# Hybrid decoder trunk on eight cores: convolution matrices cast in DRAM, the finished tile stored and reloaded in pairs of blocks, four transposes moved by one score

## The chip, the cores and the metric

The kernel runs on all 8 cores of one Trainium2 chip. Each core computes one of the 8 sequences of the batch and exchanges nothing with the others. The metric is the device time of the slowest core in microseconds (us), from its first to its last instruction with what lies around it. On each core TensorE (PE in the profile) multiplies matrices, VectorE (DVE), ScalarE (ACT) and GpSimd (POOL) work elementwise, and SyncE (SP) only issues DMAs. POOL issues DMAs too. Transfers issued by SP go through one hardware queue (q1), those issued by POOL through one software queue (q0); only the latter can change the type on the way, as from float32 to bfloat16.

## The reference

```python
def mixer_block(u, w_in, conv_a_w, conv_b_w, conv_b_bias, ln_b_g, ln_b_b, w_out):
    z = jnp.einsum("bsd,de->bse", u, w_in)
    b_a, c_a, h_a, v_b, g_b = jnp.split(z, [D_A, 2 * D_A, 3 * D_A, 3 * D_A + D_B], axis=-1)
    y_a = b_a * causal_dwconv(c_a * h_a, conv_a_w)               # 3 taps
    glu = v_b * jax.nn.sigmoid(g_b)
    cb = causal_dwconv(glu, conv_b_w) + conv_b_bias              # 31 taps
    y_b = jax.nn.silu(layer_norm(cb, ln_b_g, ln_b_b))
    return jnp.einsum("bse,ed->bsd", jnp.concatenate([y_a, y_b], -1), w_out)

h = x                                                            # (8, 4096, 1024) float32
for l in range(2):
    h = h + mixer_block(rms_norm(h, norm_mix_g[l]), ...)
    h = h + memory_cross_attention(rms_norm(h, norm_x_g[l]), rms_norm(mem, norm_mem_g[l]), ...)
    h = h + sqrelu_mlp(rms_norm(h, norm_ffn_g[l]), w_up[l], w_down[l])
return rms_norm(h, final_g)
```

The attention has 4 heads over 256 memory tokens; the MLP is 4096 wide.

## The kernel before

**Tiling.** A core's 4096 positions are cut into four tiles of 1024, each of two halves `s` of 512 positions. The outer loop runs over tiles ("passes" 0 to 3), the inner one over the two layers. The residual stream of the tile lies in `h[0]` and `h[1]`, 8 blocks of 128 channels by 512 positions in float32, 2 MB each. For one tile and one layer the stages are `mixer`, `attend`, `ffn_up` and `ffn_down`.

**Mixer.** It multiplies for the gates and values (`gv_part`), for c and h (`ch_part`), in the order gv 0, ch 0, gv 1, ch 1, each 8 groups of 8 matmuls of 512 columns. After gv 1 the gated values `glu` are laid out anew by 16 small SBUF to SBUF DMAs (line 814, 8 on SP and 8 on POOL) into `glc`, in which four phases of the positions lie on the partitions; ch 1 runs beside that. Then comes the 31-tap convolution: 8 matrices of 128x2304 (the conv matrices), 144 matmuls of 256 columns, all of which read `glc`. The layer norm and SiLU follow on DVE and ACT, and their output goes back to channel order in another 16 small DMAs per half (line 865) into `ycat`; meanwhile PE does the 8 groups of b, and then the first half of the output projection (`out_half`), whose second half needs `ycat`.

**Weights.** All weights pass through a ring of 10 slots in SBUF (`ring_pump`), in the fixed order `seq`. A slot is reloaded when the PE work on it is done. The large weights are read as float32 and cast on the way by POOL's DMAs (line 442). Some matrices are prepared once, in pass 0, kept in the DRAM tensor `wbf` in bfloat16, and read from there by SP (line 448): the folded attention matrices that `setup(l)` computes, and the conv matrices. A `wbf` matrix is loaded only once its store has been issued. In pass 0 the conv matrices of layer 0 are built in SBUF by DVE out of the taps, and those of layer 1 are cast from `bands` by POOL; in both layers each matrix is then stored to `wbf` by SP (`wb_store`, line 469), right after the layout DMAs of line 814 in SP's order. These stores use two semaphores in turn, and a store waits until the one before it on its semaphore has landed.

**Order of the work.** Each engine's instructions stand in the order in which the Python code emits them, and each waits only for what it needs. `tick()` is called once per group of 8 matmuls; each tick runs one entry of the background list `bg` and one step of each unfinished `spawn`ed task. At the end of a tile `fin(s)` computes the scale `RC[s]` of the final norm and appends 8 entries to `bg`, one for each block's multiply on DVE (line 1076), and a ninth, `final_store`: it stores the 2 MB of `h[s]` in one DMA, and issues one 2 MB DMA that reloads `h[s]` with x of the next tile, which waits for the store. `fin(0)` comes at the last tick of the tile and `fin(1)` four ticks later, so these entries run in the mixer of the next tile. The first norm of the next tile does not need `h`: it reads x through two staging buffers earlier on.

**Attention.** The scores `Sc(s, i)` (8 per half, 8 matmuls of 512 columns each) go through a softmax on DVE, ACT and POOL. `Tr(s, i)` are the transposes of its result (4 matmuls of 128 columns, then a copy from PSUM to `PT`, on DVE where i is odd and on ACT where it is even). Transposes 0 to 3 need scores 0 to 3 of their half, transposes 4 to 7 need scores 4 to 7. `X(s, m)` are the 8 output groups, which read all 8 blocks of `PT` of their half; X(s, 0) waits for blocks 4 to 7 one by one. PSUM results rotate over 7 banks. The hand-written list `plan` (line 1016) sets the order.

## Time and profile before

| | us |
|---|---|
| time, median of 3 runs | 3399.99 |
| lowest, highest | 3394.83, 3403.18 |
| profiled execution, its own time | 3395.3 |
| its span, slowest core (core 0) | 3393.7 |
| spans of the 8 cores | 3381.2 to 3393.7 |

The profiled execution is 4.7 us below the median, and its time is 1.6 us more than its span. On core 0 PE is busy for 3227.1 us, DVE for 1756.5, ACT for 1416.7 and POOL for 716.7. The chain of work that ended last is PE for 84% of its length, DMA for 7% and DVE for 3%. A busy share says how full an engine is; what a change is worth is read from the places at which PE stands still, and from what ended each wait. Beside the times of each wait, the granted clock of TensorE (PEclk, 1.00 for the full 2.4 GHz and 0.50 for 1.2 GHz) tells how fast PE was allowed to run in a stretch.

### The profile page before, as it was taken

Reading aid. Unit: us, or ns where it says so; the run is one execution under the profiler, and the core shown is the slowest. Engines: PE = TensorE matmul, PEld = TensorE weight load, DVE = VectorE, ACT = ScalarE, POOL = GpSimd, SP = SyncE. Lnnn points to the kernel's source line nnn. Section 1 sums busy time; section 2 is a strip of 40 time slices with the busy share of each in tenths; the row PEclk is TensorE's granted clock in tenths of the full one; section 3 lists DMA queues with packets and bytes.
Section 4 is the critical chain, followed back from the end, with each engine's and each line's share of the span. In section 5 each row is a group of like instructions: output and inputs, shape, how many; then the busy total and the mean of one; then the engine's idle time right before and its main releaser. Section 6 shows DMA issues by size and latency. Waiting matters only on the chain.

```text
span 3393.7 us, 50732 instructions; the slowest of 8 cores (3381.2 to 3393.7 us)
## 1 busy us (share of the span) xinstructions
PE 3227.1 (95%) x15793; PEld 1550.6 (46%) x16080; DVE 1756.5 (52%) x3016; ACT 1416.7 (42%) x2821; POOL 716.7 (21%) x908
## 2 busy tenths in 40 slices
PE   5888999799998999999999999999999999999998
PEld 2535444444444444544444444454444544454443
DVE  6655324664366632574347743476436653257433
ACT  3444313563326531474333732256332653147421
POOL 1421003320033200340003400142003310034000
PEclk9999999899999999999999999999999999999999
DMA  5878744744565444444548344354456544444441
GB/s 118 170 166 152 125 77 80 182 75 75 114 174 128 77 76 78 98 119 85 100 89 221 81 79 79 83 141 75 76 115 176 124 78 79 78 101 106 78 79 57
DMA packets 135319, 361.95 MB, mean 107 GB/s; under 512 B 32272, under 2 KB 41744, under 8 KB 135056
## 3 DMA queue, kind: packets, MB, share of 16 engines
q0 software_dynamic: 64896, 222.86, 38.5%
q1 hardware_dynamic: 69616, 134.78, 12.5%
q8 instruction: 135, 2.21, 0.3%
q10 hardware_dynamic: 544, 1.05, 0.1%
q14 instruction: 128, 1.05, 0.1%
HBM read 521.68 MB, written 34.60 MB: 164 GB/s over the span
## 4 chain that ended last, share of the span: by engine, by line
PE 84%; DMA 7%; DVE 3%; issue 3%; ACT 2%; SPq 1%; POOL 0%; DVEq 0%; ACTq 0%; another core or an unknown queue 0%; POOLq 0%
PE ps L478 84%; DMA arena<-wts 2%; ACT arena L489 2%; DMA arena<-arena 2%; DMA wbf<-arena 1%; DVE arena L493 1%; DMA outT<-arena 1%; DVE arena L503 1%; DMA arena<-xT 1%; DVE arena L977 0%; SPq L814 0%; POOL arena L493 0%; DVE arena L499 0%; DVE arena L403 0%; ACT L517 0%
## 5 line engine op out<-in xcount | busy, mean ns | idle before, releaser
L478 PE MATMUL ps<-arena 128*128 128x512 bf16 (+2 forms) x15785 | 3225.8, 364 | 154.3 <-DMA arena<-arena 43.3
L478 PEld LDWEIGHTS ps<-arena 128*128 128x128 bf16 x16072 | 1549.8, 98 | 1829.3 <-issue 184.2
L493 DVE TENSOR_TENSOR arena<-arena 128x512 f32<-128x512 f32 (+1 forms) x1280 | 868.5, 689 | 708.9 <-ACT arena L489 691.8
L489 ACT ACTIVATE arena<-arena 128x512 bf16<-128x512 f32 (+5 forms) x1441 | 753.5, 575 | 1131.1 <-DVE arena L493 1069.8
L493 DVE TENSOR_TENSOR arena<-ps,arena 128x512 f32<-128x512 f32 (+1 forms) x448 | 306.5, 688 | 655.8 <-PE ps L478 587.5
L489 ACT ACTIVATE arena<-ps 128x512 f32<-128x512 f32 (+1 forms) x608 | 361.6, 595 | 618.7 <-PE ps L478 598.0
L442 POOL DMA_DIRECT2D arena<-wts x400 | 215.7, 540 | 1764.7 <-PE ps L478 1712.5
L489 ACT ACTIVATE arena<-ps,arena 128x256 f32<-128x256 f32 (+2 forms) x441 | 229.6, 535 | 181.1 <-DVE arena L499 78.9
L498 POOL TENSOR_SCALAR arena<-arena 128x256 bf16<-128x256 f32 (+1 forms) x176 | 220.3, 1255 | 284.9 <-DVE arena L493 102.7
L493 POOL TENSOR_TENSOR arena<-arena 128x512 f32<-128x512 f32 x128 | 172.2, 1352 | 346.5 <-ACT arena L489 191.1
L493 DVE TENSOR_TENSOR arena<-arena,ps 128x512 f32<-128x512 f32 x256 | 175.4, 685 | 98.1 <-PE ps L478 95.3
L503 DVE SCALAR_TENSOR_TENSOR arena<-arena 128x256 f32<-128x256 f32 (+4 forms) x336 | 170.2, 562 | 24.0 <-ACT arena L489 23.6
L507 DVE CAST arena<-ps 128x512 bf16<-128x512 f32 x112 | 76.7, 688 | 58.1 <-PE ps L478 46.1
L865 POOL DMA_DIRECT2D arena<-arena x128 | 70.3, 554 | 167.9 <-ACT arena L489 160.3
L977 DVE TENSOR_REDUCE arena<-ps 128x2 f32<-128x512 f32 x128 | 87.8, 686 | 16.6 <-PE ps L478 15.9
L498 DVE TENSOR_SCALAR arena<-arena 128x256 bf16<-128x256 f32 (+2 forms) x152 | 57.9, 384 | 30.7 <-DMA arena<-xT 15.5
L489 ACT ACT_TABLE_LOAD x27 | 34.6, 1283 | 34.7 <-DVE arena L493 16.3
L489 ACT ACTIVATION_READ_ACCUMULATOR arena<-ps,arena 128x1 f32 x256 | 49.0, 191 | 0.0
L499 DVE TENSOR_SCALAR arena<-arena 128x2 f32<-128x2 f32 x128 | 29.3, 229 | 24.5 <-ACT arena L489 11.6
L814 POOL DMA_DIRECT2D arena<-arena x64 | 35.3, 561 | 14.1 <-PE ps L478 6.8
L517 ACT ACT_TABLE_LOAD x24 | 30.8, 1283 | 0.4
L990 DVE RECIPROCAL arena<-arena 128x2 f32<-128x2 f32 x128 | 20.4, 160 | 14.4 <-ACT arena L489 14.2
(14 smaller groups left out, 43.9 us busy)
## 6 DMA issues: line engine op xcount, KB each, us to landing
arena<-wts POOLq DMA_DIRECT2D x400, 512.0 KB, 5.5
arena<-wbf SPq DMA_DIRECT2D x64, 512.0 KB, 6.4
arena<-wbf SPq DMA_DIRECT2D x48, 576.0 KB, 4.4
arena<-xT SPq DMA_DIRECT2D x30, 512.0 KB, 5.7
outT<-arena SPq DMA_DIRECT2D x6, 2048.0 KB, 10.2
arena<-xT SPq DMA_DIRECT2D x6, 2048.0 KB, 11.7
wbf<-arena SPq DMA_DIRECT2D x16, 576.0 KB, 5.8
wbf<-arena SPq DMA_DIRECT2D x16, 512.0 KB, 10.1
```

The lines of the kernel that those rows point to most:

```text
L442: S.op("pool", lambda e, o=slot.full[:, 0:n], s=src: e.dma_start(out=o, in_=s), reads=[h[1].r()] if 2 <= i < RING else [], writes=[slot.r( ...
L478: ins = e.matmul(ps.ap, lhsT=l_, rhs=r_, start=(first and i == 0), stop=(last and i == n - 1))
L489: return e.activation(**kw)
L493: S.op(eng, lambda e: e.tensor_tensor(out=out.ap, in0=a.ap, in1=b.ap, op=op), reads=[a, b], writes=[out])
L498: return e.tensor_scalar(out=out.ap, in0=a.ap, scalar1=s1, scalar2=None, op0=op0)
L499: return e.tensor_scalar(out=out.ap, in0=a.ap, scalar1=s1, scalar2=s2, op0=op0, op1=op1)
L503: S.op(eng, lambda e: e.scalar_tensor_tensor(out=out.ap, in0=a.ap, scalar=s, in1=b.ap, op0=op0, op1=op1), reads=[a, b] + list(extra_reads) ...
L507: S.op(eng, lambda e: e.tensor_copy(out=out.ap, in_=a.ap), reads=[a], writes=[out])
L517: S.op("act", lambda e, c=c: e.activation(out=dummy.full[:, c:c + 1], in_=dummy.full[:, 0:1], func=func), reads=[dummy.r(0, 1)], writes=[])
L814: items.append((lambda e, o=o, i_=i_: e.dma_start(out=o, in_=i_), [glu.ref(None, 0, 4 * TT, (a,))], [glc.ref(None, 4 * a * glc.stride, (4 ...
L865: items.append((lambda e, o=o, i_=i_: e.dma_start(out=o, in_=i_), [yb.refs(None, [(g * CW + s * TAU, g * CW + (s + 1) * TAU) for g in rang ...
L977: S.op("dve", lambda e, o=mx.ap, i_=p3.ap: e.tensor_reduce(out=o, in_=i_, axis=AX.X, op=ALU.max), reads=[p3], writes=[mx])
```

## The change

**Conv matrices.** The host now packs `bands` for both layers. In pass 0, from the start of `ffn_up` of layer l, eight background entries 8 ticks apart issue a POOL DMA each (`band_cast`), which casts one conv matrix of the other layer from `bands` in DRAM to `wbf` in DRAM. Those of layer 1 are so cast in layer 0's `ffn_up`, those of layer 0 in layer 1's. The 16 stores by `wb_store` are gone, and layer 1 of pass 0 loads its conv matrices from `wbf` through SP, as the later passes do. Layer 0 of pass 0 still builds its own with DVE.

**The tile's end.** A background entry now multiplies two blocks and stores those two (512 KB). The eight reloads, of two blocks each, are entries of their own behind all the stores, one a tick.

**The transposes.** In `plan`, Tr(0, 3) stands behind Sc(1, 0), Tr(0, 4) to Tr(0, 6) behind Sc(1, 2), and Tr(0, 7) behind Sc(1, 3), right ahead of X(0, 0).

```diff
         def conv_id(ti, l, i):
-            if ti:
-                return b_id(l, W_CONV + i)
-            return ("c", (l - 1) * 8 + i) if l else ("d", i)
+            return b_id(l, W_CONV + i) if ti or l else ("d", i)
...
+        def band_cast(l, i):
+            cid = l * NWB_L + W_CONV + i
+            S.op("pool", lambda e: e.dma_start(out=wbf[cid], in_=bands[l * 8 + i]),
+                 writes=[Ref(None, "wbf", cid, cid + 1)], dma_sem=sem[f"bc{i}"])
+            wb_ready.add(cid)
...
                 slot = ring_get(conv_id(ti, l, cc))
-                if ti == 0:
-                    wb_store(l * NWB_L + W_CONV + cc, slot.r())
...
-                    (Sc, 0, 7), (Tr, 0, 3), (Sc, 1, 0), (Sc, 1, 1), (Tr, 0, 4), (Tr, 0, 5), (Sc, 1, 2), (Tr, 0, 6), (Tr, 0, 7),
-                    (Sc, 1, 3), (X, 0, 0), (Sc, 1, 4), (X, 0, 1), (Tr, 1, 0), (Sc, 1, 5), (X, 0, 2), (Tr, 1, 1), (Sc, 1, 6),
+                    (Sc, 0, 7), (Sc, 1, 0), (Tr, 0, 3), (Sc, 1, 1), (Sc, 1, 2), (Tr, 0, 4), (Tr, 0, 5), (Tr, 0, 6),
+                    (Sc, 1, 3), (Tr, 0, 7), (X, 0, 0), (Sc, 1, 4), (X, 0, 1), (Tr, 1, 0), (Sc, 1, 5), (X, 0, 2), (Tr, 1, 1), (Sc, 1, 6),
...
-        def final_store(ti, s):
+        def final_store(ti, s, i):
             t0 = ti * TT + s * T
-            S.op("sp", lambda e: e.dma_start(out=outT3[:, :, t0:t0 + T], in_=h[s].r3(0, 8).ap),
-                 reads=[h[s].r()], dma_sem=sem[f"o{s}"])
-            if ti + 1 < ntiles:
-                n0 = (ti + 1) * TT + s * T
-                S.op("sp", lambda e: e.dma_start(out=h[s].r3(0, 8).ap, in_=xT3[:, :, n0:n0 + T]),
-                     writes=[h[s].r()], dma_sem=sem[f"xh{s}"])
+            S.op("sp", lambda e: e.dma_start(out=outT3[:, 2 * i:2 * i + 2, t0:t0 + T], in_=h[s].r3(2 * i, 2 * i + 2).ap),
+                 reads=[h[s].r3(2 * i, 2 * i + 2)], dma_sem=sem[f"oc{s}{i}"])
+
+        def reload(ti, s, i):
+            n0 = (ti + 1) * TT + s * T
+            S.op("sp", lambda e: e.dma_start(out=h[s].r3(2 * i, 2 * i + 2).ap, in_=xT3[:, 2 * i:2 * i + 2, n0:n0 + T]),
+                 writes=[h[s].r3(2 * i, 2 * i + 2)], dma_sem=sem[f"xa{s * 4 + i}"])
...
-            for c in range(8):
-                bg.append(lambda c=c: one(c))
-            bg.append(lambda: final_store(ti, s))
+            def pair(i):
+                one(2 * i)
+                one(2 * i + 1)
+                final_store(ti, s, i)
+            for i in range(4):
+                bg.append(lambda i=i: pair(i))
+                if i % 2:
+                    bg.append(lambda: None)
+            if s == NS - 1:
+                for z in range(NS):
+                    for i in range(4):
+                        bg.append(lambda z=z, i=i: reload(ti, z, i))
...
                 lz = attend(l, await_ln)
                 if ti == 0 and l == 0 and nlayers > 1:
                     setup(1)
+                if ti == 0 and ntiles * nlayers > 1:
+                    for i in range(8):
+                        bg.append(lambda l=l, i=i: band_cast((l + 1) % nlayers, i))
+                        for _ in range(7):
+                            bg.append(lambda: None)
                 ffn_up(l)
```

SP's order in pass 0, from the layout DMAs of layer 1's mixer on (L814 before, L819 after) to the end of the SiLU layouts (L865, L868). Of before:

```order
L814 DMA arena<-arena 32x4x256 x8
L469 DMA wbf<-arena 128x2304 x5
L448 DMA arena<-wbf 128x2048
L469 DMA wbf<-arena 128x2304
L448 DMA arena<-wbf 128x2048
L469 DMA wbf<-arena 128x2304
L448 DMA arena<-wbf 128x2048
L469 DMA wbf<-arena 128x2304
L448 DMA arena<-wbf 128x2048
L865 DMA arena<-arena 32x4x128 x8
```

And of the change, where the eight stores between the two layouts are gone and eight conv loads stand ahead of the first:

```order
L447 DMA arena<-wbf 128x2304 x8
L819 DMA arena<-arena 32x4x256 x8
L447 DMA arena<-wbf 128x2048 x4
L868 DMA arena<-arena 32x4x128 x8
L447 DMA arena<-wbf 128x2048 x2
L868 DMA arena<-arena 32x4x128 x8
```

SP's order where one tile gives way to the next: stores to `outT`, reloads from `xT`, and the conv loads of the next tile (128x2304), up to the layout of `glu`. Of before:

```order
L448 DMA arena<-wbf 128x2304 x2
L1059 DMA outT<-arena 128x8x512
L1063 DMA arena<-xT 128x8x512
L448 DMA arena<-wbf 128x2304 x4
L1059 DMA outT<-arena 128x8x512
L1063 DMA arena<-xT 128x8x512
L448 DMA arena<-wbf 128x2304 x2
L814 DMA arena<-arena 32x4x256 x8
```

Of the change, where all stores come first, the last three reloads and two conv loads stand ahead of the layout:

```order
L1062 DMA outT<-arena 128x2x512
L447 DMA arena<-wbf 128x2304 x2
L1062 DMA outT<-arena 128x2x512 x5
L447 DMA arena<-wbf 128x2304 x2
L1062 DMA outT<-arena 128x2x512 x2
L1067 DMA arena<-xT 128x2x512 x5
L447 DMA arena<-wbf 128x2304 x2
L1067 DMA arena<-xT 128x2x512 x3
L447 DMA arena<-wbf 128x2304 x2
L819 DMA arena<-arena 32x4x256 x8
```

PE's order in the attention, from Tr(0, 2) to the group after Tr(0, 7); a score is 128x512 x8, a transpose 128x128 x4, and the 128x1 x4 belong to the scale of half 1. Of before:

```order
L478 MATMUL ps<-arena 128x128 x4
L478 MATMUL ps<-arena 128x512 x8
L478 MATMUL ps<-arena 128x128 x4
L478 MATMUL ps<-arena 128x512 x8
L478 MATMUL ps<-arena 128x1 x4
L478 MATMUL ps<-arena 128x512 x8
L478 MATMUL ps<-arena 128x128 x8
L478 MATMUL ps<-arena 128x512 x8
L478 MATMUL ps<-arena 128x128 x8
L478 MATMUL ps<-arena 128x512 x32
```

And of the change, where one more score stands ahead of Tr(0, 4), and Tr(0, 7) stands right ahead of X(0, 0):

```order
L483 MATMUL ps<-arena 128x128 x4
L483 MATMUL ps<-arena 128x512 x16
L483 MATMUL ps<-arena 128x1 x4
L483 MATMUL ps<-arena 128x128 x4
L483 MATMUL ps<-arena 128x512 x16
L483 MATMUL ps<-arena 128x128 x12
L483 MATMUL ps<-arena 128x512 x8
L483 MATMUL ps<-arena 128x128 x4
L483 MATMUL ps<-arena 128x512 x24
```

## Rows read from the trace of the kernel before

**Rows 1.** The page: PE's busy time, share of the span, instructions.

```profile
PE 3227.1 (95%) x15793; PEld 1550.6 (46%) x16080; DVE 1756.5 (52%) x3016; ACT 1416.7 (42%) x2821; POOL 716.7 (21%) x908
```

**Rows 2.** Whom PE waited for: us in total, times, longest us.

```profile
PE ps L478 <- DMA arena<-arena: 43.3, 5, 17.0
...
PE ps L478 <- DMA arena<-wts: 22.7, 13, 3.1
...
PE ps L478 <- DVE arena L499: 8.3, 7, 1.4
```

**Rows 3.** PE's timeline: start, us, instructions, count [idle before <-releaser].

```profile
652.80 43.01 PE L478 MATMUL ps<-arena 128*128 128x512 bf16 x208 [16.99 <-DMA arena<-arena]
...
1027.06 22.03 PE L478 MATMUL ps<-arena 128*128 128x256 bf16 x161 [10.73 <-DMA arena<-arena]
```

**Rows 4.** Stretches: us, busy (x) of PE, PEld, DVE, ACT, POOL; PEclk, DMA share, GB/s.

```profile
652.00:657.00 5.00, 4.20 (x11) 1.57 (x12) 1.21 (x2) 1.24 (x2) 0.00 (x0) 0.54 0.83 246
1027.00:1032.00 5.00, 4.94 (x24) 3.44 (x25) 0.00 (x0) 0.84 (x2) 0.33 (x1) 0.50 0.37 74
1831.00:1836.00 5.00, 4.83 (x31) 3.80 (x32) 0.00 (x0) 0.84 (x2) 0.61 (x2) 0.68 0.79 150
```

**Rows 5.** SP's timeline in layer 1 of pass 0.

```profile
593.37 13.27 SPq L469 DMA_DIRECT2D wbf<-arena  x5
...
645.19 5.74 SPq L865 DMA_DIRECT2D arena<-arena  x8
```

**Rows 6.** SP's timeline at a tile's end, and in layer 1 of the next pass.

```profile
1004.60 0.38 SPq L1063 DMA_DIRECT2D arena<-xT  x1
1005.18 0.96 SPq L448 DMA_DIRECT2D arena<-wbf  x2
1006.29 11.46 SPq L814 DMA_DIRECT2D arena<-arena  x8
...
1413.78 5.25 SPq L814 DMA_DIRECT2D arena<-arena  x8
```

**Rows 7.** More stretches, columns as in rows 4.

```profile
140.00:195.00 55.00, 35.30 (x232) 22.75 (x233) 21.17 (x33) 18.09 (x38) 13.05 (x24) 0.91 1.06 191
321.00:351.00 30.00, 29.37 (x127) 13.08 (x131) 10.36 (x15) 10.17 (x17) 1.59 (x3) 0.94 1.03 221
351.00:381.00 30.00, 29.89 (x138) 13.61 (x140) 11.81 (x18) 10.43 (x18) 2.65 (x5) 1.00 1.00 153
960.00:980.00 20.00, 19.89 (x92) 9.09 (x93) 15.79 (x24) 9.33 (x14) 5.23 (x4) 1.00 0.40 148
980.00:1004.00 24.00, 23.89 (x111) 10.89 (x112) 19.78 (x35) 7.07 (x17) 11.18 (x8) 1.00 0.81 274
```

**Rows 8.** The page's DMA issues: count, KB each, median us to landing.

```profile
arena<-xT SPq DMA_DIRECT2D x30, 512.0 KB, 5.7
outT<-arena SPq DMA_DIRECT2D x6, 2048.0 KB, 10.2
arena<-xT SPq DMA_DIRECT2D x6, 2048.0 KB, 11.7
wbf<-arena SPq DMA_DIRECT2D x16, 576.0 KB, 5.8
...
outT<-arena SPq DMA_DIRECT2D x8, 512.0 KB, 3.6
```

**Rows 9.** POOL's timeline in layer 0's `ffn_up` of pass 0.

```profile
334.44 0.53 POOL L442 DMA_DIRECT2D arena<-wts  x1 [14.26 <-PE ps L478]
...
348.25 0.53 POOL L442 DMA_DIRECT2D arena<-wts  x1 [9.83 <-PE ps L478]
```

**Rows 10.** Timelines of DVE, POOL and PE around Tr(0, 4), pass 1, layer 1.

```profile
1500.84 0.69 DVE L507 CAST arena<-ps 128x512 bf16<-128x512 f32 x1
...
1503.51 1.08 POOL L498 TENSOR_SCALAR arena<-arena 128x256 bf16<-128x256 f32 x1 [0.66 <-DVE arena L990]
...
1504.73 22.82 PE L478 MATMUL ps<-arena 128*128 128x128 bf16 x125 [1.11 <-DVE arena L499]
```

18 lines of the change are left out of this document (9 added, 9 removed).

## Prediction

> **What bounds the kernel now.** I read the page first, then PE's waits, then PE's timeline. PE is busy for 95% of the span [rows 1], so no other engine can be worth much; what can be won is the time in which PE stands still, and the time in which its clock is halved behind such a stop. PE's waits are few [rows 2]: 43.3 us on small layout DMAs, in 5 waits, 22.7 us on weights, and 8.3 us put down to DVE's L499 in 7 waits. The timeline places them [rows 3]. One layout wait of 16.99 us stands in layer 1 of pass 0. Another, of 10.73 us, stands at the end of the first tile; of the 15.6 us that are left, two waits at the ends of the second and third tile have 15.2 and the fifth wait, in the last pass's layer 1, 0.4. They are of two kinds. The first is for the SiLU layout, ahead of the second half of the output projection; the three are for the layout of `glu`, ahead of the convolution. Of the weight waits most stand in the first 200 us.
>
> The clock comes on top. Behind a stop PE goes on at a low granted clock: 0.54 over the 5 us from 652, 0.50 over those from 1027 and 0.68 over those from 1831 [rows 4], which is the lower level of 1.2 GHz for all or most of the 5 us. What is lost is 1 less the clock while PE works, not while it stands: 0.46 x 5 = 2.3 us behind the stop in pass 0, and 2.5, 1.6 and, taken as their mean, 2.0 us at the three tiles' ends, 6.1 us together. In between the clock is full.
>
> **Part 1, layer 1 of pass 0.** SP is told to store eight conv matrices between the two layouts. It issues five within 13.27 us from 593.37 on, and then the last three one by one as earlier ones land, so that L865 is issued only from 645.19 on [rows 5], just before PE goes on at 652.80. The change takes the eight stores out of SP's order. What is late next is then what rules in layer 1 of the later passes, where the same order without stores stands: there PE's wait for this layout is the fifth of rows 2, 0.4 us. So 16.99 - 0.4 = 16.6 us and the 2.3 us of clock go: **19 us**. Layer 1's conv loads move from POOL to SP, where they stand as in later passes; they are 8 issues of about 0.5 us [rows 6], behind whatever SP does in `ffn_down`, and delay nobody there.
>
> **Part 2, the start.** In layer 0 of pass 0 the stores also go. They compete with the weights of `setup(0)`: over 140 to 195 us the DMA engines are full (1.06) while PE is busy for only 35.30 of 55 us [rows 7]. A store of 576 KB lands in 5.8 us [rows 8]; eight of them hold the engines for at most some 8 x 5.8 = 46 us, but they overlap, and most are through before the weights are issued. By the rate of a full stretch, 153 GB/s [rows 7], eight conv matrices (4.7 MB) would be 31 us; stores need no float32 read and must be cheaper, and perhaps a fifth falls among the weights. I take **4 us**, between 0 and 10.
>
> **Part 3, the new casts.** Each of the 16 casts adds DMA work on POOL's queue during `ffn_up`. The trace has no DRAM to DRAM transfer. From below: 0.59 MB at 153 GB/s, the rate of a stretch in which the engines do nothing but cast weights [rows 7], is 3.9 us. From above: that cast plus a store of the same matrix, 5.8 us [rows 8], is 9.7 us. I take 5 us, nearer to the cast, since one pass of the engines does both. Two weights (1.05 MB, 6.9 us at the same rate) are needed per step of 348.25 - 334.44 = 13.8 us [rows 9], which leaves 6.9 us for one cast. At 321 us about 33 us of weights are queued, since the engines stay full until 381 (1.03 and 1.00, 60 us [rows 7]) while 8 weights, 27 us, come in. A weight issued at 334 is used 4 steps or 55 us later. Even at 9.7 us a cast the queue grows to 33 + 8 x 2.8 = 55 us, just that. So the casts are hidden: **0 us**. Their issue, some 0.5 us each (a weight's is 0.53 [rows 9]), stands between waits of POOL of 10 us.
>
> **Part 4, the tiles' ends.** Before, the second half's reload of 2 MB is issued at 1004.60, two conv loads follow, and the 16 layout DMAs start at 1006.29 behind them [rows 6]. PE is ready at 1016.3 (1027.06 - 10.73, [rows 3]) and must wait. In layer 1, with only conv loads ahead, the layouts are issued in 5.25 us and not in 11.46 [rows 6], and PE does not wait. In the change the last reload is issued 5 ticks (13.8 / 8 = 1.73 us each, 8.6 us) ahead of the layout. Is the queue empty by then? From 960 to 1004 the engines did 0.40 x 20 + 0.81 x 24 = 27.4 us of work [rows 7]; the second reload, now to be done in the same stretch, adds at most 11.7 us [rows 8]. That is 39.1 of 44 us: tight, but it fits, and the first 20 us, 60% idle before, are where the early stores go. A layout started at 1006 then has until 1016.3, and in layer 1 the issue alone needs 5.25 us. DVE's 16 multiplies are the same ones, slightly earlier, so it is no later with `glu`. I expect three waits of 0.5 us in place of 25.9: 24.4 us, and the 6.1 us of clock: **30 us**. The bounds are 0 (all stays) and 32.
>
> **Part 5, the transposes.** Tr(0, 4) waits 1.11 us in the layer shown and 8.3 us in seven of the eight layers: POOL finishes the last piece of its softmax at 1503.51 + 1.08 = 1504.59, and PE goes on at 1504.73 [rows 2, 10]. One more score, 8 matmuls or 1.7 us, now stands ahead of it, while the copy of Tr(0, 3) on DVE, 0.69 us [rows 10], may come to stand ahead of that softmax piece. So 0.7 to 1.1 us a layer go. Against that, Tr(0, 7) is now directly ahead of X(0, 0), whose last matmul needs its copy 1.5 us later; the copy stands on DVE behind Sc(1, 3)'s maximum (0.7 us) and a small operation (0.2), so it ends some 1.8 us after the transpose: 0.3 us lost a layer. Net 8 x 0.6 = **5 us**, between -5 and 9.
>
> **The sum.** 19 + 4 + 0 + 30 + 5 = 58 us off the profiled execution's 3395.3 us: 3337. All this is core 0, the slowest of that execution, but also the one with the longest waits at the tiles' ends. The spans of the eight cores lie 12.5 us apart, and another core with shorter waits there may be the slowest afterwards; I add 3 us for it. The runs' median is 4.7 us above the profiled execution, of which I add 3. I take **3343 us**.
>
> **The rivals.** (a) *The queue is not empty.* The stores and reloads are the same 8.4 MB, and my estimate leaves 5 us. Small layout pieces are also slow beside full engines: 11.46 us to issue. If half of the three waits and of their clock stays, 32 / 2 = 16 us come back: 3359. For it: 0.81 over 980 to 1004 [rows 7]. Against it: PE is ready only 10 us after the layout's start.
>
> (b) *Smaller transfers are worse.* A 2 MB store lands in 10.2 us and a 512 KB store in 3.6, four of them 14.4; a 2 MB reload in 11.7 and a 512 KB load in 5.7, four of them 22.8 [rows 8]. If these times added up, two stores and two reloads would cost 2 x 4.2 + 2 x 11.1 = 30.6 us more of the engines, 26 beyond what fits; 26 less some 4 us that the layout has to spare are 22, so at three ends 3 x 22 us of waits and 3 x 2 of clock, 72 us in place of 32, and the kernel would be at 3395.3 + 40 + 6 - 28 = 3413, the 6 being what I added above. It decides once four pieces together cost twice one whole. Against it: the pieces are issued one a tick, without waiting for each other. The Trainium skill, "DMA: Bandwidth & Descriptors", section "Rules for kernel authors", asks for at least 1 MiB per DMA, which speaks against the cut of the 2 MB transfers; no stretch of this trace shows such pieces back to back in a full queue.
>
> (c) *The casts are slow*, and this is the case that ends slower: a DMA that reads and writes DRAM in long rows may use the engines badly. Beyond 6.9 us a cast the excess piles up: 16 x (C - 6.9) less the slack of 22 us in the first layer and 55 in the second. That eats all 58 us at C = 15.3 us; at 20 us the loss is 133 us and the kernel is at 3343 + 133 = 3476. Nothing in the trace speaks for a rate three times lower than any cast in it.
>
> (d) *The transposes cost more than they give*: a full microsecond a layer at X(0, 0), and nothing at the start. The 5 us become a loss of 3, the 4 us at the start go: 3343 + 8 + 4 = 3355.
>
> **How the numbers follow.** Forecast 0.65, (a) 0.20, (d) 0.08, (b) 0.04, (c) 0.03. The range holds the forecast, its bounds, (d) and (a): from 3325, with 32 us at the tiles' ends, 9 by the transposes, 10 at the start and none of the 6 us added, to 3367, 8 us past (a). What a measurement can tell from no change is about 0.3%, 10 us. Part 1 alone is worth 19, so faster is 0.92; same 0.02 for a mix of (a), (b) and (d), slower 0.06.
>
> **What would show it.** Right: SP's L819 and L868 of pass 0, layer 1 without stores between them and PE's 17 us gone; at the tiles' ends no layout wait over 1 us and PEclk 1.00 from 1000 to 1100; PE without weight waits in pass 0's `ffn_up`; at Tr(0, 4) no wait over 0.4 us. Wrong: a wait on `arena<-arena` of several us at the tiles' ends (a, b), waits on `arena<-wts` between 321 and 600 us (c), or a new wait on DVE's L507 cast ahead of the last matmul of X(0, 0) (d).

## The result and the profile after

The changed kernel takes **3352.5 us** (median of its runs), against 3398.4 us for the kernel before in the same session; the ratio is **0.986, with a 95% interval of 0.984 to 0.988**, so it is faster by 1.4%. The prediction was 3343 us within 3325 to 3367. On a second chip the same kernel had a median of 3342.6 us against 3392.9 before, ratio 0.985 (0.981 to 0.990). So the gain is 46 us on the first chip and 50 on the second, where the forecast had 57 from its median of 3399.99. On these chips a whole die sometimes runs for hundreds of microseconds at a lowered clock, with any kernel; executions in which that happened are left out of all comparisons.

The profiled execution took 3348.1 us; its slowest core is now core 1, with a span of 3346.6 us. The page of that core, first PE's line, then three of the DMA issues (KB each, us to landing):

```profile
PE 3248.9 (97%) x16080; PEld 1550.4 (46%) x16080; DVE 1756.6 (52%) x3016; ACT 1416.4 (42%) x2821; POOL 718.3 (21%) x916
...
arena<-xT SPq DMA_DIRECT2D x54, 512.0 KB, 9.4
outT<-arena SPq DMA_DIRECT2D x32, 512.0 KB, 4.0
wbf<-bands POOLq DMA_DIRECT2D x16, 576.0 KB, 17.1
```

PE is busy for 97% of the span, where [rows 1] had 95%. Whom PE waited for (us in total, times, longest), to be read beside [rows 2]:

```profile
PE ps L483 <- DMA arena<-wts: 22.9, 13, 2.9
...
PE ps L483 <- POOL arena L503: 1.8, 4, 1.1
...
PE ps L483 <- DMA arena<-arena: 0.7, 2, 0.5
```

The waits on layout DMAs fell from 43.3 us, on core 0, to 0.7 on this core, which had 41.1 before. The waits on weights are what they were. SP's timeline in layer 1 of pass 0 (start, us, instruction, count) shows why, beside [rows 5]: between the layout of `glu` and that of the SiLU there are no stores, only four loads of prepared attention matrices (128x2048 in SP's order above), and the last eight pieces are issued at 631.86 and not at 645.19.

```profile
582.70 5.24 SPq L819 DMA_DIRECT2D arena<-arena  x8
...
605.35 6.23 SPq L447 DMA_DIRECT2D arena<-wbf  x4
622.30 6.28 SPq L868 DMA_DIRECT2D arena<-arena  x8
628.79 0.92 SPq L447 DMA_DIRECT2D arena<-wbf  x2
631.86 5.96 SPq L868 DMA_DIRECT2D arena<-arena  x8
```

PE's timeline in that layer has a stop of 0.20 us where [rows 3] has 16.99, and at the first tile's end it goes through `glu`'s layout without a stop, where there were 10.73 us (core 1 itself had 19.13 and 8.29 us there):

```profile
640.72 7.07 PE L483 MATMUL ps<-arena 128*128 128x512 bf16 x32 [0.20 <-DMA arena<-arena]
...
984.81 29.75 PE L483 MATMUL ps<-arena 128*128 128x512 bf16 x209
```

**A third level of the clock.** The kernel before, in its profiled execution, had the granted clock at full speed or at half of it, the latter only behind a stop. Now there are short stretches at 0.81, with PE working and no stop ahead of them. Stretches on core 1 (us, busy of PE, PEld, DVE, ACT, POOL; PEclk, DMA share, GB/s): the second and the fourth are two of them, the first and the third lie on either side of the second. The last line is the second stretch once more, on core 0:

```profile
1408.00:1417.00 9.00, 8.80 (x43) 3.91 (x42) 7.29 (x14) 3.88 (x7) 0.00 (x0) 1.00 1.02 228
1417.00:1422.00 5.00, 5.00 (x21) 2.13 (x20) 4.65 (x9) 4.56 (x12) 1.58 (x3) 0.83 0.98 292
1422.00:1432.00 10.00, 10.00 (x48) 4.47 (x47) 7.92 (x13) 6.95 (x19) 5.01 (x10) 0.99 0.56 168
...
2216.00:2222.00 6.00, 6.00 (x25) 2.51 (x24) 4.69 (x8) 5.85 (x16) 2.69 (x5) 0.82 0.80 240
...
1417.00:1422.00 5.00, 5.00 (x21) 2.06 (x19) 4.66 (x8) 2.89 (x8) 1.77 (x5) 0.82 0.61 157
```

In 5 us PE starts 21 matmuls and not 24. Cores 0 and 1 have 16 such stretches of 3.7 to 7.5 us, at the same times in both, 84 us in all; the share of the clock that was withheld in them adds up to 15.7 us. Cores 2 and 3 have 13 (12.4 us withheld), and each core of the other die has one of 15 us (2.8 us). These sums are the most that the level can have cost: where PE would have waited anyway, a lower clock costs nothing. From the first tile's end to the second's, where PE hardly waits, four of the stretches withheld 3.5 us, and cores 0 and 1 took 3.6 and 2.8 us longer than in the second chip's execution of the same kernel below, which has no such stretch. Over the whole span, cores 0 to 3 are only 2.9 to 7.9 us longer than there, with other starts and other waits.

### The profile page after: what moved, and what is told of

Its sections match the earlier page's. It is cut to its first block, busy times and chain, and to the rows that moved or that the text cites. A ratio compares the mean times of both kernels' runs of the same rounds, so it can differ in the third digit from the quotient of the medians.

```text
span 3346.6 us, 51116 instructions; the slowest of 8 cores (3331.7 to 3346.6 us)
## 1 busy us (share of the span) xinstructions
PE 3248.9 (97%) x16080; PEld 1550.4 (46%) x16080; DVE 1756.6 (52%) x3016; ACT 1416.4 (42%) x2821; POOL 718.3 (21%) x916
## 4 chain that ended last, share of the span: by engine, by line
PE 91%; DVE 3%; DMA 3%; issue 2%; ACT 2%; POOL 0%; DVEq 0%; ACTq 0%; SPq 0%; POOLq 0%
PE ps L483 91%; DMA arena<-wts 2%; ACT arena L494 2%; DVE arena L498 1%; DVE arena L508 1%; DMA arena<-xT 1%; DVE arena L980 0%; POOL arena L498 0%; DVE arena L402 0%; DMA arena<-arena 0%; ACT L522 0%; ACT L494 0%; POOL arena L503 0%; POOL arena L868 0%; DVE arena L993 0%
## 5 line engine op out<-in xcount | busy, mean ns | idle before, releaser
L508 DVE SCALAR_TENSOR_TENSOR arena<-arena 128x256 f32<-128x256 f32 (+3 forms) x336 | 169.5, 564 | 27.7 <-ACT arena L494 27.3
L868 POOL DMA_DIRECT2D arena<-arena x128 | 70.1, 552 | 196.9 <-ACT arena L494 188.6
L494 ACT ACT_TABLE_LOAD x27 | 34.6, 1283 | 35.0 <-DVE arena L498 18.5
L819 POOL DMA_DIRECT2D arena<-arena x64 | 35.3, 562 | 16.9 <-PE ps L483 14.0
## 6 DMA issues: line engine op xcount, KB each, us to landing
wbf<-bands POOLq DMA_DIRECT2D x16, 576.0 KB, 17.1
```

Of the source, the lines that this page charges most:

```text
L494: return e.activation(**kw)
L508: S.op(eng, lambda e: e.scalar_tensor_tensor(out=out.ap, in0=a.ap, scalar=s, in1=b.ap, op0=op0, op1=op1), reads=[a, b] + list(extra_reads) ...
L819: items.append((lambda e, o=o, i_=i_: e.dma_start(out=o, in_=i_), [glu.ref(None, 0, 4 * TT, (a,))], [glc.ref(None, 4 * a * glc.stride, (4 ...
L868: items.append((lambda e, o=o, i_=i_: e.dma_start(out=o, in_=i_), [yb.refs(None, [(g * CW + s * TAU, g * CW + (s + 1) * TAU) for g in rang ...
```

## The experiments

### The parts of the change, one at a time

These three and the kernel before ran in one session, in which the kernel before had a median of 3397.8 us.

**The kernel before, once more.** No edit; it asks whether the 0.81 level belongs to the change.

> The kernel before, unchanged, with a profile on the same chip as the three parts. In the trace of the changed kernel the cores of one die show a granted clock of 0.81 in 12 to 16 short stretches of 4 to 8 us while PE works without a stop, and the other die shows one of 15 us; the trace of before had none. Theory A (the denser kernel causes them): none here, or as few as one. Theory B (the chip or the execution causes them): a similar number here, 10 or more on one die, and a ratio of 1.00 all the same.

It has no time to compare, but its trace answers the question: core 0 of the kernel before ran for 885 us at this level. Fifty microseconds of it (columns as above):

```profile
2800.00:2850.00 50.00, 49.65 (x188) 20.73 (x191) 16.63 (x24) 14.23 (x24) 3.17 (x6) 0.81 0.39 64
```

So the level itself is not a product of the change; whether its short stretches are, the next execution of the changed kernel tells, below. DMA engines at 0.39 here, and at 0.98 in the stretch of the changed kernel, also tell that a full DMA queue is not needed for it. Before its clock fell, at 2621 us, this core waited for the layouts at the tiles' ends only 1.9, 4.6 and 3.7 us, where the first trace of the same kernel has 10.7, 7.2 and 8.1; cores 4 to 7 waited 5.5 to 7.6 us. So these waits scatter from execution to execution.

**Conv matrices alone.** The casts, and no stores; tile ends and transposes as before.

```diff
-                if ti == 0:
-                    wb_store(l * NWB_L + W_CONV + cc, slot.r())
...
+                if ti == 0 and ntiles * nlayers > 1:
+                    for i in range(8):
+                        bg.append(lambda l=l, i=i: band_cast((l + 1) % nlayers, i))
+                        for _ in range(7):
+                            bg.append(lambda: None)
```

> Before, with part 1 alone: conv matrices cast DRAM to DRAM in pass 0, no stores by SP; 2 MB stores and reloads and the old order of transposes. My account of the prediction: the 17 us wait in pass 0, layer 1 gone with 2 us of clock, 0 to 5 us at the start, nothing lost in ffn_up: 17 to 24 us less than before, ratio 0.993 to 0.995; waits of 7 to 11 us at the three tiles' ends as before. Rival (the casts cost PE time): less than 15 us, with waits on weights in ffn_up of pass 0.

Measured: 3375 and 3367 us, two executions, 27 us under the kernel before by their mean and above the 17 to 24 that I had expected. In the first, which was profiled, cores 0 and 1 ran at 0.81 for 148 us of the start. Core by core in its trace, the stretch from the end of layer 1's convolution in pass 0 to the start of the next layer's is 18.5 us shorter in the mean of the eight cores, and that from layer 0's convolution to layer 1's 5.4 us: 24 us. PE's waits on core 0:

```profile
PE ps L483 <- DMA arena<-arena: 28.1, 7, 8.4
...
PE ps L483 <- DVE arena L504: 8.3, 7, 1.4
```

The long wait of pass 0 is gone, the three at the tiles' ends are left (8.4 the longest), and so is the one at the transposes. This is the gain of the prediction's parts 1 and 2, and no loss to the casts is seen beside it.

**Tiles' ends alone.** Pairs of blocks, and the reloads behind the second stream's stores.

```diff
-            for c in range(8):
-                bg.append(lambda c=c: one(c))
-            bg.append(lambda: final_store(ti, s))
+            for i in range(4):
+                bg.append(lambda i=i: pair(i))
+                if i % 2:
+                    bg.append(lambda: None)
+            if s == NS - 1:
+                for z in range(NS):
+                    for i in range(4):
+                        bg.append(lambda z=z, i=i: reload(ti, z, i))
```

> Before, with part 2 alone: stores in pairs of blocks, and the eight reloads behind all the stores. My account: the three waits at the tiles' ends fall from 26 us (core 0) to under 2 us, with 6 us of clock: 24 to 32 us less, ratio 0.991 to 0.993; the 17 us wait in pass 0, layer 1 stays. Rival (the clock of 0.81 takes the gain back): a gain under 20 us, with 10 or more stretches at 0.81 on one die.

Measured: 3375.2 us, ratio 0.9935 (0.9918 to 0.9953), 22.6 us less, a little under the 24 to 32 expected. Of the layout waits on core 0 the one of pass 0 is left, and the other four together have 3.4 us:

```profile
PE ps L478 <- DMA arena<-arena: 23.2, 5, 19.8
```

In the mean of the cores the three ends are shorter by 9.0, 7.5 and 8.3 us, clock included: 24.8 us, of which 4 come back at the start and in layer 1 of pass 0. Together with the casts' 24 to 27 us this is 47 to 50, and the whole change gave 46 us on one chip and 3392.9 - 3342.6 = 50.3 on another: as far as these times can tell, the two parts add up.

**Transposes alone.**

```diff
-                    (Sc, 0, 7), (Tr, 0, 3), (Sc, 1, 0), (Sc, 1, 1), (Tr, 0, 4), (Tr, 0, 5), (Sc, 1, 2), (Tr, 0, 6), (Tr, 0, 7),
-                    (Sc, 1, 3), (X, 0, 0), (Sc, 1, 4), (X, 0, 1), (Tr, 1, 0), (Sc, 1, 5), (X, 0, 2), (Tr, 1, 1), (Sc, 1, 6),
+                    (Sc, 0, 7), (Sc, 1, 0), (Tr, 0, 3), (Sc, 1, 1), (Sc, 1, 2), (Tr, 0, 4), (Tr, 0, 5), (Tr, 0, 6),
+                    (Sc, 1, 3), (Tr, 0, 7), (X, 0, 0), (Sc, 1, 4), (X, 0, 1), (Tr, 1, 0), (Sc, 1, 5), (X, 0, 2), (Tr, 1, 1), (Sc, 1, 6),
```

> Before, with part 3 alone: the order of transposes. By the traces the wait at Tr(0, 4) of 1.1 us a layer falls to some 0.4 us of smaller waits: 4 to 6 us less, ratio 0.998 to 0.999, PE's waits for DVE's L499 gone. Rival (d) of the prediction: X(0, 0) waits about 1 us for the copy of Tr(0, 7) in each layer, ratio 1.000 to 1.001.

Measured: ratio 1.0005 (0.9984 to 1.0026). The time can't tell 5 us from nothing here: five executions lie at 3391 to 3394 us, three at 3408 to 3411 with a mean clock of 0.98 on one pair of cores, and their median, 3392.9, is 4.9 us under the kernel before. The trace can tell where PE stops: PE's waits no longer name the small operation on DVE that had 7 waits in [rows 2]. In each layer the stop of 1.1 us at Tr(0, 4) is replaced by one of at most 0.3 us, with one of 0.38 us behind Tr(0, 7) in two layers, while the next stop, 0.74 us at the transposes of the second stream, stays. At the tiles' ends, where nothing was changed, this trace is together 8 us shorter in the mean of the cores than the first trace of the kernel before; with the scatter seen above, that can't be put down to the transposes.

### Rivals put to the test on the changed kernel

These four ran on the second chip, where the kernel before had a median of 3392.9 us.

**The changed kernel, once more.** No edit.

> The changed kernel once more, unchanged, in another execution. In its first profiled execution the cores 0 to 3 showed a granted clock of 0.81 in 13 to 16 stretches of 4 to 8 us each, 12 to 16 us lost, which the kernel before did not show. Theory A, these stretches are made by this kernel's denser matmuls: they come again on all cores of die 0 at the same places (971, 1418, 2216 and 2569 us), 12 to 16 us lost again, and the span of the slowest core is again 3346 us. Theory B, they belong to the chip or the execution: their number and places differ, and where they are few the slowest span is 3332 to 3340 us and the ratio to the kernel before 0.982. Theory C, they are a feature of die 0 alone: cores 4 to 7 again have one at most.

Measured: 3342.6 us (3340.9 to 3344.9), ratio 0.985. Theory B holds: no core of either die had a single stretch at 0.81. Core 0 is 3393.7 - 3335.4 = 58.3 us shorter than in the profile of the kernel before, where the sum of the prediction was 58; but in the mean of the eight cores it is 50.4. Core 0 was the slowest of the profile that the prediction read, by waits that scatter from execution to execution, and among the executions of the kernel before its span varies by 20 us and more (3376 to 3398 us in the session of the three parts). The longest layout wait left on core 0 is 2.4 us, at the second tile's end:

```profile
PE ps L483 <- DMA arena<-wts: 16.9, 11, 2.6
...
PE ps L483 <- DMA arena<-arena: 5.1, 5, 2.4
```

Core 4 has one of 4.2 us at the first tile's end, and half clock behind it. Here are SP's and PE's timelines there, and the stretch (columns as above):

```profile
979.13 10.09 SPq L819 DMA_DIRECT2D arena<-arena  x8
```

```profile
994.93 1.44 PE L483 MATMUL ps<-arena 128*128 128x256 bf16 x6 [4.17 <-DVE arena L508]
```

```profile
994.00:1000.00 6.00, 5.07 (x24) 3.51 (x25) 0.75 (x2) 0.84 (x2) 1.11 (x3) 0.50 0.73 114
```

The releaser named, a DVE multiply, need not be the cause: PE waits here for several things, and the records name the one that came last, while SP needs 10.09 us for pieces that take it 5 to 6 in layer 1 and the first pieces land at 994.6. Core 4 is the slowest of that execution, 3343.3 us, 7.9 above core 0.

**Reloads behind the layout.** 13 empty steps ahead of them.

```diff
             if s == NS - 1:
+                for _ in range(13):
+                    bg.append(lambda: None)
                 for z in range(NS):
```

> The changed kernel with 13 empty steps ahead of the reloads, so that all eight reloads of x are issued behind the layout of glu at the end of a tile, and not just ahead of it. What the prediction's part 4 says, that the layout waited because reloads stood ahead of it in the queue: the layout then has an even emptier queue, PE waits 0 us at glu's layout of the three ends; the reloads of 4 MB come in during the convolution and could only delay the layout of the SiLU, by at most 1 to 2 us a place, since 8 reloads of 9 us landing overlap. Expected time equal to the changed kernel within 3 us. Rival, the queue is full there anyway: the waits of 8 to 10 us come back at the SiLU layout, with 2 us of clock each, and the time is 25 to 35 us above the changed kernel.

Measured: 3372.4 us, ratio 0.9943 (0.9925 to 0.9962), 30 us above the changed kernel. The rival holds and my own expectation was wrong: the waits move one layout further. PE's and SP's timelines on core 0 at the first tile's end:

```profile
1040.87 4.36 PE L483 MATMUL ps<-arena 128*128 128x512 bf16 x11 [10.43 <-DMA arena<-arena]
```

```profile
1021.24 9.87 SPq L868 DMA_DIRECT2D arena<-arena  x8
1031.33 2.15 SPq L447 DMA_DIRECT2D arena<-wbf  x2
1033.62 5.51 SPq L868 DMA_DIRECT2D arena<-arena  x8
```

Eight pieces of a layout take 9.87 us to issue behind the reloads, where they take 6.28 in layer 1 of pass 0 above. The other two ends have 9.0 and 7.8 us. So what the change found is a gap long enough ahead of a layout: 4 MB of reloads cost 8 to 10 us on this core at whichever layout follows them too closely.

**Whole transfers.** The same steps, but 2 MB at once, at the step of the last pair.

```diff
         def final_store(ti, s, i):
+            if i < 3:
+                return
...
-            S.op("sp", lambda e: e.dma_start(out=outT3[:, 2 * i:2 * i + 2, t0:t0 + T], in_=h[s].r3(2 * i, 2 * i + 2).ap),
+            S.op("sp", lambda e: e.dma_start(out=outT3[:, :, t0:t0 + T], in_=h[s].r3(0, 8).ap),
...
         def reload(ti, s, i):
+            if i < 3:
+                return
...
-            S.op("sp", lambda e: e.dma_start(out=h[s].r3(2 * i, 2 * i + 2).ap, in_=xT3[:, 2 * i:2 * i + 2, n0:n0 + T]),
+            S.op("sp", lambda e: e.dma_start(out=h[s].r3(0, 8).ap, in_=xT3[:, :, n0:n0 + T]),
```

> The changed kernel, but at the ends of the tiles each stream is stored in one transfer of 2 MB and reloaded in one transfer of 2 MB, each at the step where the changed kernel issues its last pair; the place of the last issue is the same, only the cut into pairs is undone. If the cut is what gives the gain (the early stores spread over the slack), the whole transfers are still in the queue when the layout starts: a wait of 3 to 8 us on the layout at each of three ends, 15 to 30 us more in all with the clock. If the place of the reload ahead of the layout is what gives it and the cut nothing, the time is that of the changed kernel within 3 us. If smaller transfers are worse, as rival (b) has it, this kernel is faster than the changed one.

Measured: 3351.5 us, one execution only, 9 us above the changed kernel, between the two expectations. The profiled execution agrees on cores 0 to 3, which ran at full clock: they are at 3346 to 3351 us, 9 to 15 above the same cores of the changed kernel. The wait at the first end on core 0, and the issues ahead of it:

```profile
994.90 5.33 PE L483 MATMUL ps<-arena 128*128 128x256 bf16 x32 [4.38 <-DMA arena<-arena]
```

```profile
956.49 0.53 SPq L1071 DMA_DIRECT2D arena<-xT  x1
961.30 2.05 SPq L447 DMA_DIRECT2D arena<-wbf  x2
966.59 0.38 SPq L1071 DMA_DIRECT2D arena<-xT  x1
973.38 3.77 SPq L447 DMA_DIRECT2D arena<-wbf  x2
978.91 7.57 SPq L819 DMA_DIRECT2D arena<-arena  x8
```

The waits at the twelve ends of those cores are 0.7 to 5.1 us. So the place of the reload, ahead of the layout by several steps, is worth some 55 to 65% of the gain at the ends, and the cut into pairs the rest. That the cut helps because the first pairs go out while the queue still has room is my reading; no run parts it from the pieces' size. Rival (b) is refuted. The Trainium skill, "DMA: Bandwidth & Descriptors", "Rules for kernel authors", asks for at least 1 MiB per DMA where the most bandwidth is the goal; here, where a small transfer must land soon behind them, four pieces of 512 KB did better than one of 2 MB, so the measurement decides against it for this place.

**Twice the casts.** 16 more of them, of the same matrices to a tensor nobody reads, each half way between two of the 16.

```diff
                         bg.append(lambda l=l, i=i: band_cast((l + 1) % nlayers, i))
-                        for _ in range(7):
+                        for _ in range(3):
+                            bg.append(lambda: None)
+                        bg.append(lambda l=l, i=i: extra_cast((l + 1) % nlayers, i))
+                        for _ in range(3):
                             bg.append(lambda: None)
```

> The changed kernel with 16 more casts DRAM to DRAM in pass 0, of the same matrices to a scratch tensor that nobody reads, each 4 steps behind one of the 16 that are needed: it doubles the cost in dispute. From the engines' share of the two kernels one cast takes 2.5 to 3.7 us of the DMA engines, against room for 6.9 us per cast interval, so two take 5.0 to 7.4 us. If so, the doubled casts are still nearly hidden: 0 to 4 us on the time, and the DMA share of 321 to 431 us rises from 1.02 only by what is not yet full, with no or one short wait on weights. If instead a cast holds the engines for the 9.7 us of the prediction's upper bound, 16 of them are 155 us more than the room: waits on weights in the up projection of pass 0 of 60 us or more, and as much on the time.

Measured: 3356.3 us, ratio 0.9897 (0.9873 to 0.9921), 13.7 us above the changed kernel, so neither of the two expectations was right. Two stretches of core 0, which cover each layer's up projection and what follows it, first of the kernel before, then of the changed kernel, then of this one:

```profile
290.00:580.00 290.00, 280.95 (x1349) 134.52 (x1374) 111.62 (x168) 83.80 (x141) 38.64 (x61) 0.99 0.63 110
```

```profile
290.00:580.00 290.00, 283.39 (x1361) 132.55 (x1359) 111.57 (x169) 84.35 (x142) 42.20 (x63) 1.00 0.75 129
690.00:980.00 290.00, 288.95 (x1351) 131.27 (x1350) 136.97 (x211) 105.70 (x182) 41.56 (x60) 1.00 0.67 138
```

```profile
290.00:580.00 290.00, 277.62 (x1330) 129.80 (x1328) 109.12 (x164) 82.53 (x140) 41.19 (x67) 0.99 0.90 142
690.00:980.00 290.00, 284.99 (x1331) 129.12 (x1329) 135.43 (x210) 108.47 (x192) 39.65 (x62) 0.99 0.83 136
```

The first eight casts add 0.12 x 290 = 35 us of the engines, 4.4 us each; the extra eight add 0.15 x 290 / 8 = 5.4 in layer 0 and 0.16 x 290 / 8 = 5.8 in layer 1. The 2.5 to 3.7 us that the expectation used came from stretches which the casts' work had overrun, or in which the engines were full. At 5.4 us a cast, two of them need 10.8 us where 6.9 are free: the queue grows, and PE waits for weights at 456.76 (1.30 us) and 473.95 (2.77 us), just where the queue of layer 0 used to be worked off. In the mean of the cores 8.7 us are lost there, and another 5.0 in layer 1, at a stop of 2.0 to 4.5 us near 896 us:

```profile
456.76 3.61 PE L488 MATMUL ps<-arena 128*128 128x512 bf16 x16 [1.30 <-DMA arena<-wts]
460.66 10.52 PE L488 MATMUL ps<-arena 128*128 128x512 bf16 x48 [0.28 <-DMA arena<-wts]
473.95 15.66 PE L488 MATMUL ps<-arena 128*128 128x512 bf16 x64 [2.77 <-DMA arena<-wts]
```

### More reloads' places, and the other transposes

These four ran on a third chip. There the kernel before had a median of 3414 us, and the granted clock of its first die was 0.977 to 0.984 in the executions compared, against 0.987 to 0.991 on the second chip. All four kernels traced there have the 0.81 level in 12 to 26 stretches a core; of the kernel before there is only the mean clock. So times compare among these four and the kernel before on that chip alone, and even there with care.

**Four empty steps** ahead of the reloads, and **reloads of the first stream earlier** by four steps.

```diff
             if s == NS - 1:
+                for _ in range(4):
+                    bg.append(lambda: None)
                 for z in range(NS):
```

```diff
-                bg.append(lambda i=i: pair(i))
+                if s == NS - 1:
+                    bg.append(lambda i=i: (reload(ti, 0, i), pair(i)))
+                else:
+                    bg.append(lambda i=i: pair(i))
...
-                for z in range(NS):
-                    for i in range(4):
-                        bg.append(lambda z=z, i=i: reload(ti, z, i))
+                for i in range(4):
+                    bg.append(lambda i=i: reload(ti, NS - 1, i))
```

> The changed kernel with four empty steps ahead of the eight reloads at the end of a tile: the last reload is issued one step ahead of the layout of glu in place of five, some 7 us later. With 13 empty steps, where all reloads came behind that layout, PE waited 7.8 to 10.4 us at the SiLU layout of each end and the time was 30 us above the changed kernel. Theory A, what counts is whether the queue of 4 MB of reloads has drained when a layout starts: here four or more reloads are still in it, so PE waits 5 to 10 us at glu's layout of each of three ends and the time is 20 to 35 us above the changed kernel. Theory B, only the issue on SP counts, a reload behind which the layout must be issued: one reload's issue is 0.6 us, and the time is that of the changed kernel within 3 us.

> The changed kernel, with the reloads of the first stream issued one by one beside the last four pairs of the second stream and not behind them, so that the last reload is issued four steps, some 7 us, earlier. In the changed kernel PE still waits up to 3 us for glu's layout at the ends of the tiles on some cores (2.4 us on core 0, 3.0 on core 4 at the first end of its second profile). Theory A, the queue is not quite drained there: these waits fall below 0.5 us, and the time falls by 2 to 5 us. Rival, the engines are full over the whole stretch and an earlier issue changes nothing, or the reloads collide with the weights of the last down projection: no gain, or new waits on weights ahead of the layout, up to 5 us slower.

(The waits of 2.4 and 3.0 us that this names are those of the kernel with twice the casts; the changed kernel's are 2.4 us on core 0, at the second end, and 4.2 on core 4.)

Measured: 3387 us with the delay, ratio 0.9937 (0.9904 to 0.9969), and 3383 us with the earlier reloads, ratio 0.9911 (0.9891 to 0.9931). By the waits, the delay's theory A is wrong: at the three ends seven of the eight cores wait 0.8 us at most for `glu`'s layout and one waits 2.1 once, so for these waits one step of room is as good as five. The earlier reloads do take these waits to nothing on all eight cores, the longest left on a layout being 1.2 us behind the convolution. Yet neither is fast. For the delay that is not explained: by its time and ratio it is some 24 to 30 us worse than the changed kernel, which theory A had foretold, but the traced execution has no such waits, and 87 to 98 us of withheld clock on cores 0 to 3, most of it in stretches of 128 to 155 us far from the tiles' ends. With the earlier reloads the clock is seen. Here is core 0, where the reloads run:

```profile
956.00:971.00 15.00, 14.91 (x57) 6.20 (x57) 13.11 (x27) 4.18 (x12) 4.32 (x4) 0.81 0.98 293
```

A stretch of 15.1 us at 0.81 costs 2.8 us, about what the wait had cost. This kernel has 14 of them on cores 0 and 1 and 17 on cores 2 and 3 (40 and 48 us withheld); on core 0 one stands among the reloads of each end, at 956, 1757 and 2559 us. The waits that were looked for went, and the clock took time back.

**The other stream's transposes**, alone and with the earlier reloads.

```diff
-                    (X, 0, 3), (Tr, 1, 2), (Sc, 1, 7), (X, 0, 4), (Tr, 1, 3), (X, 0, 5), (Tr, 1, 4), (Tr, 1, 5), (X, 0, 6),
-                    (Tr, 1, 6), (Tr, 1, 7), (X, 0, 7)] + [(X, 1, m) for m in range(8)]
+                    (X, 0, 3), (Tr, 1, 2), (Sc, 1, 7), (X, 0, 4), (Tr, 1, 3), (X, 0, 5), (X, 0, 6), (Tr, 1, 4), (Tr, 1, 5),
+                    (Tr, 1, 6), (X, 0, 7), (Tr, 1, 7)] + [(X, 1, m) for m in range(8)]
```

> The changed kernel, with the transposes 4 to 7 of the second stream one step later as well: ahead of transpose 4 stands X(0, 6) too. In the changed kernel PE stops once per layer for 0.74 to 0.75 us at the transposes of that stream, in seven layers, and for 1.1 us in the last. If the stop is there because the softmax piece ends after PE is through with X(0, 5), the 16 matmuls that now stand ahead of it hide it: 8 x 0.75 = 6 us less. Rival: the stop moves to where the transposes now stand directly ahead of what uses them, X(0, 7) and X(1, 0), with the copies on DVE 0.7 us behind: 0 us, or up to 3 us more.

> The two edits together, the earlier reloads of the first stream and the later transposes of the second. If both theories hold, the time is 8 to 11 us under the changed kernel, near 3333 us where that is at 3343; if only one does, 3 to 6 us under it; if neither, the same time.

Measured: 3361.6 us alone, ratio 0.9848 (0.9829 to 0.9868), and 3370.5 us with both, ratio 0.9879 (0.9857 to 0.9900). So on this chip the earlier reloads, added to the later transposes, cost 9 us; cores 2 and 3, the slowest in both traces, have 19 stretches at 0.81 with them and 16 without, 54 and 45 us withheld. PE's timeline of the changed kernel, and of this one, across the same transposes of the next pass:

```profile
1089.75 6.39 PE L483 MATMUL ps<-arena 128*128 128x512 bf16 x37
1096.88 28.30 PE L483 MATMUL ps<-arena 128*128 128x128 bf16 x140 [0.74 <-DVE arena L498]
```

```profile
1059.82 15.30 PE L483 MATMUL ps<-arena 128*128 128x512 bf16 x93
1075.36 44.90 PE L483 MATMUL ps<-arena 128*128 128x512 bf16 x227 [0.24 <-DVE arena L993]
```

The stop of 0.74 us is gone in every layer, and that of 1.1 us in the last one too, on all eight cores: 7 x 0.74 + 1.1 = 6 us. This is the fastest kernel of its session. But core 0 still has 34 us of its clock withheld, in 12 stretches of this kind:

```profile
1402.00:1417.00 15.00, 14.70 (x75) 7.14 (x75) 12.96 (x23) 8.97 (x20) 1.28 (x3) 1.00 0.97 221
1417.00:1432.00 15.00, 15.00 (x58) 6.19 (x57) 9.65 (x16) 12.72 (x30) 9.40 (x16) 0.81 0.47 135
```

58 matmuls start in 15 us, after 75. The changed kernel did not run on this chip, so by time it is not shown that the later transposes beat it; the ratios to the kernel before, 0.985 for these and 0.985 to 0.986 for the changed kernel, are the same. That they take stops away is shown, that they take time away is not.

## Why the prediction was right

**What bounds the kernel, part 1 and part 4** stood on the layout waits and on the half clock behind them, and both went as told. Part 1, 19 us: measured 18.9 us in the mean of the eight cores of the second execution, with 0.6 us of a transpose in it. Part 4, 30 us on core 0: 29.5 us (13.3, 6.2 and 10.0) in the second execution and 30.4 (12.3, 8.8 and 9.3) in the first, and 25 to 27 in the mean of the cores, since core 0 had the longest waits. The estimate that 39.1 us of work fit into 44 was right but close: in the second execution waits of up to 4.2 us are left, in the first up to 1.5. Rival (a), half of the waits coming back, did not occur.

**Part 2, 4 us** between 0 and 10: from the start to layer 1's convolution 4.5 us in the mean of the cores of the second execution, 10 on core 0. The 10 are not all the change's: with the transposes alone, where nothing was changed at the start, core 0 was already 5.6 us ahead there and the mean of the cores 0.5 behind.

**Part 3, 0 us.** Right, and for the reason given: 4.4 to 5.8 us a cast where I took 5. The row that misleads is the landing: 17.1 us, since a cast is queued behind weights; the engines' share gives its cost. Rival (c)'s formula held for one layer and not for the other. At 10.8 us for two casts the excess is 8 x 3.9 = 31 us a layer. In layer 0, with 22 us of slack, it gives 9 us, and 8.7 were lost; in layer 1, with 55, it gives nothing, and 5.0 were lost. So the 55 us of slack for the second layer were not all there.

**Part 5, 5 us**: the term that was mis-sized. The stops at Tr(0, 4) shrank from 1.1 to at most 0.3 us, as told, but in the second execution all that lies outside parts 1, 2 and 4 gave only 2 us, to which come some 1.2 that stand inside their stretches: 3 us in all. With the transposes alone the eight attentions together are 3.8 us shorter in the mean of the cores. Against the move I had put 0.3 us a layer at X(0, 0), for a copy on DVE; a stop stands there in two of the eight layers only, of 0.38 us, and it is for a copy on ACT. So the move cost less than I had allowed and also gave less; where the rest went stays open.

**The 3 + 3 us added at the end** are the step that failed. I expected another core, not slowed by the waits, to be 3 us above core 0, and the sum read on core 0 to hold otherwise. In the first execution core 1 was 7.6 us above it. The 0.81 level is not the reason, since cores 0 and 1 had the same 16 stretches at the same times. Most of it stood before the tiles' ends were reached: by the same short stop in layer 1 of pass 0, first on core 0 and then on core 1, they are 6.5 us apart.

```profile
673.06 17.20 PE L483 MATMUL ps<-arena 128*128 128x512 bf16 x90 [0.38 <-ACT arena L494]
...
679.53 10.72 PE L483 MATMUL ps<-arena 128*128 128x512 bf16 x54 [0.38 <-ACT arena L494]
```

In the profile before it was the other way round: PE began layer 1's convolution at 600.1 us on core 0 and at 593.7 on core 1, now at 589.7 and 595.2. What ended first or last at the start changed places between the executions, and with it the slowest core. So the gain read on the slowest core of one profile, 58 us, was too high for the kernel: against that profile the mean of the cores gained 50 in both executions. In the first, the 0.81 level took some part of 15.7 us from both cores besides; no term of mine had it.

In the second execution no such stretch occurred; core 4 was 7.9 us above core 0, by 2.4 us at the start, its waits of 4.2 and 1.8 us at two ends and the half clock behind the first, and the median was 3342.6 us. That the forecast of 3343 was met to 0.4 us there is luck: the kernel before stood at 3392.9 us on that chip and at 3399.99 where the forecast began, and the gain was 50 us and not 57. The other core was worth 5 us more than I had added, the 3 for the median nothing.

## What to carry to other kernels

A small transfer that PE needs soon should find the queue nearly empty: here 4 MB of reloads cost 8 to 10 us at whichever layout followed them too closely, and 0 to 4 where they were cut into pieces, begun as the data was ready and issued some steps ahead. Judge a new DMA by what it adds to the engines' share over a stretch long enough to hold all of it, not by its landing; and double it on the chip before you trust the slack. Read a gain on all cores and not on the slowest one alone: the slowest of one execution is partly so by chance. Once PE is busy for 97%, a forecast needs room for the granted clock: the microseconds that a removed stop gives can be taken back by it.

## What the runs showed of the hardware

The granted clock has a third level of 0.81 besides the full one and the half. It came in short stretches (3.7 to 7.9 us in the changed kernel's first execution), for 15.1 us at a time (on the third chip's first die with the earlier reloads and with the later transposes), and for hundreds of us (885 on core 0 of the kernel before). It came to pairs of cores at the same time, on one die and not on the other, with PE working and no stop ahead of it. It depends on the chip or the execution more than on the kernel: the same kernel had 15.7 us of clock withheld by it on core 1 in one execution and none on any core in the other. The Trainium skill, "TensorE: Matmul & The Clock Gate", "Seeing it yourself", describes such a state, 13/16 of the clock, 0.8125, once three cores of a die run dense matmuls, and says that it holds while the load lasts. The traces agree on the level. They don't on the rest: here PE is busy for 96 to 97% on all four cores of both dies, and the level holds for 5 us or 15 or not at all. What starts and ends a stretch stays open. The 15 us stretches often stand some 10 us behind the end of a convolution, where the matmuls of 512 columns have begun again (622, 1022, 1417, 1819, 2215, 2620 and 3016 us on core 0 with the later transposes), but that was not tried by itself.

Withheld clock is not lost time: with the conv matrices alone cores 0 and 1 ran at 0.81 for 148 us of the start, 28 us withheld, and reached layer 1's convolution 6 us later than the mean of the other six.
